# Sums for two norms built beside w_out_2, a plain fp32 group, and a new order of weight pieces

## The reference, cut to what matters

```
y = concat(y_a, y_b, y_c) @ w_out_2                 # 2048 x 2048
x = x + rms_norm(y, norm_mix_post_2)
h = rms_norm(x, norm_ffn_pre_2)
up = causal_conv3(h @ w_up_2) + conv_ffn_bias_2     # 2048 x 11264
f = (silu(gate half of up) * value half) @ w_down_2 # 5632 x 2048
x = x + rms_norm(f, norm_ffn_post_2)
```

## Time and profile before

| what | value |
|---|---|
| median of 3 runs | 2777.91 us |
| the profiled execution, its own time | 2782.62 us |
| its span, first to last instruction | 2780.4 us |
| mean granted TensorE clock | 0.973 of full speed |
| TensorE matmul busy | 2631.0 us, 95% |
| VectorE, ScalarE busy | 1657.2 us (60%), 1158.8 us (42%) |

### The profile page before, as it was taken

The page is one execution under the profiler, slowest core; times in us unless marked ns, Lnnn a source line. Parts: engine busy times, 40 slices in busy tenths (PEclk is TensorE's granted clock), DMA queues, the critical chain, the costliest instruction groups (busy, mean ns, idle before and its releaser), DMA issues.

```text
span 2780.4 us, 43313 instructions
## 1 busy us (share of the span) xinstructions
PE 2631.0 (95%) x19304; PEld 2473.3 (89%) x19304; DVE 1657.2 (60%) x1961; ACT 1158.8 (42%) x1291; POOL 11.2 (0%) x24
## 2 busy tenths in 40 slices
PE   7899999999998999999999999849699999999998
PEld 4488799899998999999999999839599989998996
DVE  4266676477776645545445667964456655664665
ACT  3332555334334434434334543323354434443444
POOL 0000000000000000000000000000000000000000
PEclk9899999999998999999999999969799999999999
DMA  9775665378775755555555554414245555555453
GB/s 375 306 260 212 212 216 200 131 281 285 296 268 190 255 180 184 184 186 184 185 183 182 180 188 164 151 61 167 76 167 182 182 193 184 184 182 191 173 182 121
DMA packets 77226, 547.81 MB, mean 197 GB/s; under 512 B 8848, under 2 KB 8976, under 8 KB 12272
## 3 DMA queue, kind: packets, MB, share of 16 engines
q1 hardware_dynamic: 74304, 533.53, 54.4%
q0 software_dynamic: 2448, 11.01, 1.0%
q10 hardware_dynamic: 288, 0.50, 0.1%
HBM read 539.77 MB, written 5.24 MB: 196 GB/s over the span
## 4 chain that ended last, share of the span: by engine, by line
PE 85%; DVE 8%; ACT 3%; DMA 2%; issue 1%; SPq 0%; POOL 0%; DVEq 0%; ACTq 0%
PE acc L271 22%; PE acc L275 21%; PE acc L273 21%; PE acc L291 4%; PE acc L292 4%; PE acc L293 4%; DVE cacc L1277 2%; DVE wlo L239 2%; DMA raw<-in_w_mod 2%; PE mp L468 1%; PE mp L293 1%; PE mp L291 1%; PE mp L292 1%; PE mp L342 1%; DVE macc L386 1%
## 5 line engine op out<-in xcount | busy, mean ns | idle before, releaser
L239 DVE TENSOR_TENSOR wlo<-raw,whi 128x1024 fp32r<-128x1024 f32 x813 | 983.6, 1223 | 841.1 <-ACT whi L229 839.2
L229 ACT ACTIVATE whi<-raw 128x1024 fp32r<-128x1024 f32 x813 | 851.7, 1057 | 1292.8 <-PE acc L275 984.4
L271 PE MATMUL acc<-hh,whi 128*128 128x256 f32 x3616 | 1035.9, 286 | 30.5 <-DVE wlo L239 16.8
L273 PE MATMUL acc<-hl,whi 128*128 128x256 f32 x3616 | 1026.3, 284 | 0.0
L275 PE MATMUL acc<-hh,wlo 128*128 128x256 f32 x3616 | 1026.3, 284 | 0.0
L271 PEld LDWEIGHTS acc<-hh,whi 128*128 128x128 f32 x3616 | 696.0, 192 | 42.9 <-issue 23.2
L273 PEld LDWEIGHTS acc<-hl,whi 128*128 128x128 f32 x3616 | 696.3, 193 | 1.3 <-issue 1.0
L275 PEld LDWEIGHTS acc<-hh,wlo 128*128 128x128 f32 x3616 | 695.9, 192 | 0.0
L271 PE MATMUL acc<-mh,whi 128*128 128x256 f32 x1536 | 436.2, 284 | 16.5 <-DVE ml L1357 15.1
L273 PE MATMUL acc<-ml,whi 128*128 128x256 f32 x1536 | 435.7, 284 | 0.0
L275 PE MATMUL acc<-mh,wlo 128*128 128x256 f32 x1536 | 435.6, 284 | 0.0
(11 more groups left out here) (278 smaller groups left out, 2059.2 us busy)
## 6 DMA issues: line engine op xcount, KB each, us to landing
raw<-in_w_in SPq DMA_DIRECT2D x98, 1024.0 KB, 4.9
raw<-in_w_mod SPq DMA_DIRECT2D x96, 1024.0 KB, 5.3
raw<-in_w_up SPq DMA_DIRECT2D x88, 1024.0 KB, 4.9
raw<-in_w_mlp_in SPq DMA_DIRECT2D x64, 1024.0 KB, 4.9
raw<-in_w_mlp_out SPq DMA_DIRECT2D x64, 1024.0 KB, 4.9
raw<-in_w_down SPq DMA_DIRECT2D x44, 1024.0 KB, 4.9
raw<-in_w_out SPq DMA_DIRECT2D x32, 1024.0 KB, 5.0
raw<-in_w_fourier_out SPq DMA_DIRECT2D x8, 1024.0 KB, 5.7
```

Of the source, the lines that this page charges most:

```text
L229: nc.scalar.activation(whi[:, r, :], raw_slot(k)[:, 2 * GC * j:2 * GC * (j + 1)], ACT.Copy)\
L239: nc.vector.tensor_tensor(wlo[:, r, :], raw_slot(k)[:, 2 * GC * j:2 * GC * (j + 1)], whi[:, r, :].bitcast(f32), ALU.subtract).then_inc(S[" ...
L271: nc.tensor.matmul(dst, whi[:, r, cols], hi[:, kt, :], start=begin, stop=False, skip_group_check=True)
L273: nc.tensor.matmul(dst, whi[:, r, cols], lo[:, kt, :], start=False, stop=False, skip_group_check=True)
```

## The change

1. *First norm in sums.* While w_out_2 runs, each group's squares are taken as soon as it is evicted and added by TensorE in the middle of the next group (`y_sum`); the last group's are squared straight out of the accumulator, in two halves.
2. *Second norm in sums.* With r the first norm's factor, g its gain and y the product, the new x is x + r g y, and the sum of its squares is (sum x^2) + 2 r (sum x g y) + r^2 (sum g^2 y^2). `product` and ScalarE's squares with a scale make the two new terms, `fold` adds them up, `zz_sums` sums them over the features on TensorE, and (sum x^2) is kept in `sx` from the norm before w_in_2. The second norm's factor is applied to the accumulator when a w_up_2 group is evicted (`um1`, `um2`), not to h.
3. *Plain fp32.* The first w_up_2 group multiplies the raw weights (four slots of the new kind "f") with `hf`, h without the second factor, in plain fp32 (`plain_group`). hh and hl are made from `hf` for all later groups.
4. *Order of weight pieces.* `ffn_pair` makes one piece after the read of the accumulator, one after the taps and 6 at its end, in place of 8 ahead of it. The accumulator is free after one VectorE operation.
5. *Places.* hh and hl lie elsewhere in SBUF; `sx`, `um1`, `um2`, `xy`, `yy`, `hf` are new.

The core of the diff:

```diff
-STREAM += "d" * (MLP_CHUNKS * 32 - 16 + 34 + 16 + 22 * 4 + 44)
+STREAM += "d" * (MLP_CHUNKS * 32 - 16 + 34 + 16 + 2) + "ffff" + "d" * (2 + 20 * 4 + 44)
...
+        def plain_group(pe, st, i, h, frees, each, between):
+            acc_wait(pe, st, i, frees)
+            for s, k in enumerate(FSLOT):
+                slot_in(pe, k)
+                between(s)
+                for j in range(4):
+                    kt = 4 * s + j
+                    each(kt)
+                    for t in range(4):
+                        last = nc.tensor.matmul(acc[i][:, t * NT:(t + 1) * NT],
+                                                raw_slot(k)[:, j * GC + t * P:j * GC + (t + 1) * P], h[:, kt, :],
...
+                last.then_inc(S["f_used"], 1)
...   # ScalarE
-            for g in range(0, 4):
-                C(st)
-            all_read(act, F_OUT2)
-            norm_squares(act, 2, yT)
-            norm_root(act, 2, mp[0])
-            act.wait_ge(S["vt_ok"], 4)
-            norm_squares(act, 3, xT2)
-            norm_root(act, 3, mp[0])
-            apply_act(act, LO_MIX, [(hh, None, lambda kt: pcol("norm_ffn_pre_2", kt), None, 4 * q, 4)
-                                    for q in range(4)])
-            act.wait_ge(S["lo_ok"], LO_MIX + 4)
+            for n in range(4):
+                C(st)
+                i = 1 - n % 2
+                if n < 3:
+                    act.wait_ge(acc_free[i], F_U[i] + n // 2 + 1)
...
+                    nc.scalar.activation(tiles(tmp[:, n % 2, :]), yT[:, 4 * n:4 * n + 4, :], ACT.Square)\
+                        .then_inc(S["y_sq"], 1)
+                else:
+                    group_done(act, st)
+                    act.wait_ge(S["yq_ps"], 2)
+                    for half in range(2):
+                        cols = slice(half * GC, (half + 1) * GC)
+                        nc.scalar.activation(tmp[:, 1, cols], acc[i][:, cols], ACT.Square).then_inc(S["y_sq"], 1)
+                    act.wait_ge(S["yq_ps"], 5)
+                    nc.scalar.activation(root[:, :], mp[0][:, 0:NT], ACT.Sqrt, bias=eps[:, 0:1], scale=1.0 / D)\
+                        .then_inc(S["y_rt"], 1)
+                    act.wait_ge(acc_free[i], F_U[i] + n // 2 + 1)
+                if n:
+                    act.wait_ge(S["yy_ok"], n)
+                for t in range(4):
+                    last = nc.scalar.activation(um2[:, t, :], yT[:, 4 * n + t, :], ACT.Square,
+                                                scale=pcol("norm_mix_post_2", 4 * n + t))
+                last.then_inc(S["gy_sq"], 1)
+            for i, (a, n) in enumerate(N2_JOBS):            # jobs of 2, 2, 4, 4, 4 tiles
+                act.wait_ge(S["xm_ok"], i + 1)
+                for kt in range(a, a + n):
+                    last = nc.scalar.activation(hf[:, kt, :], xT2[:, kt, :], ACT.Copy,
+                                                scale=pcol("norm_ffn_pre_2", kt))
+                last.then_inc(S["hf_ok"], 1)
+                act.wait_ge(S["hf_ok"], i + 1)
+                nc.scalar.activation(hh[:, a:a + n, :], hf[:, a:a + n, :], ACT.Copy).then_inc(S["fh_ok"], 1)
...   # ScalarE, ffn_pair, for v in range(2)
-                    C(st)
-                    group_done(act, st)
+                    if n < v:
+                        C(st, 7, met=8)
+                    elif n:
+                        st.e += 8
+                    if n + v:
+                        group_done(act, st)
+                        hi_piece(act, st)
+                    act.wait_ge(acc_free[v], F_OUT2[v] + n + 2 * c + 1)
...                   # bias and tap, now from um
+                    if n + v:
+                        hi_piece(act, st)
...                   # sigmoid, or the copy to mh
+                    if n + v:
+                        C(st, 4 if n + v == 11 else 6, met=0)
...   # VectorE, w_out_2
+            for n in range(4):
+                C()
+                group_done(dve, st)
+                i = 1 - n % 2
+                if n == 3:
+                    dve.wait_ge(S["y_sq"], 5)
+                nc.vector.tensor_copy(yT[:, 4 * n:4 * n + 4, :], tiles(acc[i][:, :])).then_inc(acc_free[i], 1)
+                dve.wait_ge(acc_free[i], F_U[i] + n // 2 + 1)
+                if n:
+                    dve.wait_ge(S["xy_ok"], n)
+                product(n)                                  # 4 x um1 = y * gain * x
+                if n < 3:
+                    fold(xy, um1, n == 0, "xy_ok")          # 2 adds of 128x512 (1 for n == 0)
+                    dve.wait_ge(S["gy_sq"], n + 1)
+                    if n:
+                        dve.wait_ge(S["yy_ok"], n)
+                    fold(yy, um2, n == 0, "yy_ok")
+            dve.wait_ge(S["y_rt"], 1)
+            own(nc.vector.reciprocal(rstd[:, 0, :], root[:, :]))
+            for i, (a, n) in enumerate(N2_JOBS):
+                own(nc.vector.tensor_tensor(tiles(tmp[:, i % 2, 0:n * NT]), yT[:, a:a + n, :], rbc(0, n), ALU.mult))
+                for t in range(n):
+                    x = xT2[:, a + t, :]
+                    last = nc.vector.scalar_tensor_tensor(x, tmp[:, i % 2, t * NT:(t + 1) * NT],
+                                                          pcol("norm_mix_post_2", a + t), x, ALU.mult, ALU.add)
+                last.then_inc(S["xm_ok"], 1)
...                   # the last folds, hl = hf - hh job by job, the second factor from zz_sums
...   # VectorE, ffn_pair: C and group_done as on ScalarE, then
+                    nc.vector.tensor_tensor(um[:, :, :], tiles(acc[v][:, :]), rbc(1), ALU.mult)\
+                        .then_inc(acc_free[v], 1)
+                    if n + v:
+                        lo_piece(dve, st)
...                   # taps, now from um
+                    if n + v:
+                        lo_piece(dve, st)
...                   # products, ml
+                    if n + v:
+                        C(4 if n + v == 11 else 6, met=0)
...   # TensorE
+            def y_sum(n):
+                pe.wait_ge(S["y_sq"], n + 1)
+                ones_sum(pe, mp[0][:, 0:NT], tmp[:, n % 2, :], n == 0, False).then_inc(S["yq_ps"], 1)
+            for n in range(4):
+                mm_feature(pe, st, 1 - n % 2, mh, ml, 1, ready=lambda s: y_sum(n - 1) if n and s == 2 else None)
...                   # two halves of two matmuls for the last group; then
+            plain_group(pe, st, 0, hf, 1, hf_each, zz_sums)  # zz_sums: 4 matmuls before the fourth slot
...
-                        mm_feature(pe, st, v, hh, hl, 0, ready=h_ready(pe, LO_MIX),
-                                   free=(S["cd_ok"], 2 * (4 * c + p) - 1 + v) if p else None)
+                        if c + p + v:
+                            mm_feature(pe, st, v, hh, hl, 1, ready=split if c + p == 0 else None)
                 for g in range(4):
-                    if g < 2:
-                        pe.wait_ge(S["cd_ok"], 2 * (4 * c + pairs) - 1 + g)
-                        st.f[g] += 1
-                    else:
-                        acc_wait(pe, st, g % 2, 1)
+                    acc_wait(pe, st, g % 2, 1)
```

More of the change, by code:

```diff
@@ L204, in load @@
                         sp.wait_ge(S["mod_acc"], n_mod - EARLY)
+                    elif c == "f":
+                        sp.wait_ge(S["f_used"], before.count("f"))
                     else:
@@ L1358, in _ @@
                                     ALU.subtract).then_inc(S["mxl_ok"], 1)
[L1359 to L1377, removed]
@@ L1378, in _, with fold @@
-            dve.wait_ge(S["x1_ok"], KT)
[L1379 to L1382, removed]
+            dve.wait_ge(S["x1_ok"], KT)
+            def fold(total, part, first, sem):
+                flat = part[:, :, :].rearrange("p t n -> p (t n)")
+                if first:
+                    nc.vector.tensor_tensor(total[:, :], flat[:, 0:GC], flat[:, GC:2 * GC], ALU.add)\
+                        .then_inc(S[sem], 1)
+                else:
+                    own(nc.vector.tensor_tensor(total[:, :], total[:, :], flat[:, 0:GC], ALU.add))
+                    nc.vector.tensor_tensor(total[:, :], total[:, :], flat[:, GC:2 * GC], ALU.add)\
+                        .then_inc(S[sem], 1)
@@ new lines, in product @@
+            def product(n):
+                for t in range(4):
+                    last = nc.vector.scalar_tensor_tensor(um1[:, t, :], yT[:, 4 * n + t, :],
+                                                          pcol("norm_mix_post_2", 4 * n + t), xT2[:, 4 * n + t, :],
+                                                          ALU.mult, ALU.mult)
+                own(last)
+            for n in range(4):
[15 more added lines that the diff above has]
+                    fold(yy, um2, n == 0, "yy_ok")
@@ new lines, in _ @@
+            fold(xy, um1, False, "xy_ok")
+            dve.wait_ge(S["gy_sq"], 4)
+            dve.wait_ge(S["yy_ok"], 3)
+            fold(yy, um2, False, "yy_ok")
+            for i, (a, n) in enumerate(N2_JOBS):
+                dve.wait_ge(S["fh_ok"], i + 1)
```

(35 more changed lines are left out.)

68 lines of the change are left out of this document (46 added, 22 removed).

## The result

The changed kernel takes 2751.2 us (median of 4 runs, 2740.28 to 2753.26) against 2777.69 (2776.43 to 2779.68): -26.5 us, ratio 0.99 with a 95% interval of 0.9885 to 0.9916. The forecast was 2759.2, range 2750 to 2767. But, as the runs show, some 10 us of the 26.5 come from a term that the prediction had at nothing: the new places of hh, hl and what lies behind them in SBUF. The sum is wrong there, and its total came near for another reason than the one worked out.

What follows compares the result with a forecast made beforehand. TensorE, busy 95% of the span, was taken to bound the kernel. Closing the gap behind w_out_2 (-24.9), w_down_2 stops (+7.5) and removed waits (-1.3) gave -18.7 us: 2777.9 to 2759.2, range 2750 to 2767.

Steps and rivals of the forecast that it cites:

- the stops: TensorE waits about ten times for VectorE's down_add in and behind w_down_2, 0.62 to 0.78 us each: 7.5 us more.
- The hole: Between w_out_2's end and the first w_up_2 group's end, 71.3 us shrink to 46.4, sums in w_out_2 included: -24.9 us.
- Start at T' + 9.5: The first w_up_2 matmul starts 9.5 us after w_out_2's new end (T'), where it was 46.1 after the old.
- group 0: The first w_up_2 group, in plain fp32 with half clock and zz_sums, lasts 31.7 us.
- the half clock: At the first w_up_2 group, TensorE runs 4.6 us at half clock after its pause, losing 2.3 us.
- the two old stops: Waits at the first w_down_2 piece of chunks 0 and 1, 1.3 us together, go away.
- hh and hl moved: New SBUF places of hh and hl change no instruction: 0 us.
- The new order of pieces: Weight pieces between eviction steps gain nothing in w_up_2 and remove two late-piece waits at w_down_2: -1.3 us.
- A: Rival: the w_down_2 stops are not there, giving -26.2 us, 2751.7; chance 0.13.
- B: Rival: the gap behind w_out_2 closes less, losing 4 to 9 us of the gain, 2763 to 2768; chance 0.13.
- C: Rival: each of ten new w_down_2 stops drops the clock, costing 2.3 us each, +4.3 in all, 2782; chance 0.04.
- D: Rival: the change is neutral, TensorE's added 11.5 us meeting a gap smaller than it looked; chance 0.02.

Runs made afterwards that it cites:

- h1: The changed kernel with 96 unused bytes ahead of hh, distance 0 as in the kernel before: 2761.0 us, ratio 0.9955.
- f4: The kernel before with 32 unused bytes ahead of whi, moving weights and activations together: 2779.4 us in one execution.
- h2: h1 with the first w_up_2 group through split weight pieces instead of plain fp32: 2761.9 us, ratio 0.9952.
- f1: The kernel before with 160 unused bytes behind wlo, giving the changed kernel's distance: 2768.2 us in one execution.
- e3: The changed kernel, with VectorE evicting each w_down_2 unit before making its 8 (6) weight pieces: 2737.0 us.
- e4: The changed kernel with the old order of weight pieces, all 8 ahead of each eviction: 2804.0 us, ratio 1.010.
- h3: e3 with 32 unused bytes ahead of hh, distance -64: 2704.9 us, ratio 0.975.

## Why the prediction was wrong, and where it was right

*What the change does at a fixed place.* Before and after at the same distance: 2775.1 and 2761.0 at 0 (-14.0), 2768.2 (one execution) and 2751.2 at -96 (-17), 2728.5 and 2711.0 at -64 (-17.5). Only the pair at 0 was timed in one series; at -64, where the kernel before also ran in 2705.0 once, the difference is worth little. Forecast: -18.7. The mechanism was right, and one term was too small: the stops.

*The hole.* In h1, at the pace of the kernel before, w_out_2 lasted 99.3 us instead of 94.5: +4.8, forecast 5.2. From its end to the first w_down_2 matmul it took 202.8 us instead of 232.9: -30.1, and the forecast's two terms (24.9 + 5.2) are 30.1. Start at T' + 9.5, group 0 (32.0 us in the changed kernel, forecast 31.7), the second norm's factor and group 1 all came as worked out; only the half clock lasted 1 us longer.

*The stops.* From the first w_down_2 matmul to the last matmul, h1 took 576.9 us, the kernel before 567.7: +9.1, forecast +6.2 (7.5 - 1.3). All ten stops came where they were counted. (With +4.8 and -30.1 this makes -16.2; h1's profiled execution also began w_out_2 5.1 us earlier than that of the kernel before. f4 and h2, at the same pace, began it 2.9 and 2.6 earlier, so single executions differ by some us there.) TensorE's waits in h1:

```profile
PE acc L299 <- DVE yN L1535: 1.8, 2, 0.9
...
PE acc L279 <- DVE yN L1535: 1.6, 2, 0.9
```

A stop was worked out as idle time, 0.78 us, but the matmul behind it starts 1.27 us after the last one, where 0.23 is the rule, and the next one follows 0.33 to 0.34 later: 1.15 us for a stop in front of a w_down_2 unit. The ten together come to 11.2 us, forecast 7.5, and the two old stops, counted in the same way, had cost 1.8 and not 1.3. That is the missing 3 us. The prediction's "some 10 if a semaphore's way costs 0.2 more each" was its upper end; that is near what happened.

*hh and hl moved: "no instruction changes; 0".* This is the step that failed: a term put at nothing, because the instructions stay the same. (mh, ml, ch and cl moved by the same 96 bytes.) What the runs showed in its place is a change of pace in every stage, 0.1200 to 0.1187 us for each 128x256 pass and 0.2267 to 0.2333 for each 128x512 pass. f1 gives it alone: -6.5 us in one pair of runs; by the medians it is 26.5 less some 14 to 17.5, so 9 to 12.5 us. Part of the changed kernel's w_up_2 ran at 0.1173 instead of 0.1187 for no reason in its instructions. Whether such second paces also make its executions spread (13 us, h1's 6) is not shown: seven executions of the kernel before spread over 10.5 us in one series, and those of e3, at -96 too, over 5.5. The trace of the kernel before could not warn of this by itself: a pass of 256 columns took 0.1200 us in every stage, and every stage had the same distance.

*The new order of pieces.* I gave it -1.3 for the late pieces and held that there was nothing to gain in w_up_2, since TensorE never waits there. That is true of the old eviction only; e4 shows that with the new one the order is worth 53 us, half clocks included. The forecast's total was unharmed because I had worked out the new order's own timing rightly (no wait in any w_up_2 group).

*The rivals.* A (no stops) is refuted by the ten stops, although its number, 2751.7, is nearly the median: right by accident. B is refuted: the hole closed as worked out. C (the stops cost the clock) is refuted. The microsecond of the changed kernel in which TensorE stood at 2203 us (PEclk is the last column but two):

```profile
2203.00:2204.00 1.00, 0.20 (x2) 0.04 (x1) 0.91 (x1) 0.80 (x1) 0.00 (x0) 1.00 0.99 418
```

The granted clock stayed at 1.00 through every one of the stops, from 1972 us to the last one at 2717. The Trainium skill's passage on PSUM cycling (TensorE: Matmul & The Clock Gate, "A second HAM failure mode: psum-queue depth-cycling") did not come true for stops of 0.8 us, some 19 us or more apart. e4, with waits of up to 3.2 us, did show such a swing of the clock, so rival C's mechanism exists in this kernel, but not at this length of stop. D is refuted by h1's interval.

*Open.* Why the distance modulo 256 sets the pace, why there are two paces at -64, -96 and 128, and what switches between them. That each pace is a fixed number of cycles shared by reads of weights and of activations is a guess that no run tested. Whether hh and hl or mh and ml could have distances of their own was not tried.

## What to carry to other kernels

Before working out a change of a kernel that TensorE bounds, read the distance between two matmuls and hold it against another placement: 32 bytes of padding between weights and activations took off 31 us of 2775 here, more than the change that this document is about did; the change, a distance of -64 and the other order of evictions together took off 70. Compare two programs only at equal places, or a tensor that moved will pass for the idea. And when an eviction gets a step more, count again when the next piece of work behind it on the same engine is due.

## What the runs showed of the hardware

The distance of fp32r passes of 128x256 ran from 0.1133 to 0.1200 us at full granted clock, and that of 128x512 passes from 0.2267 to 0.2343, with the distance in SBUF of the two operands modulo 256 bytes and, at a given distance, between two values (h3: 427 and 444 records in 50 us of one execution). The best place for 128x512 (0) was among the worst for 128x256. A TensorE stop of 0.9 us on a semaphore cost 1.15 (h1), and left the granted clock at 1.00; behind waits of 1.8 to 3.2 us it fell to half for 3.4 us ten times (e4). A plain fp32 group of 64 matmuls and one of 192 fp32r passes were worth the same here, 2761.0 against 2761.9 us, since the plain one is slower and needs less beforehand.
